# The fourth token sum split by quarters, and the down weights loaded through ScalarE's queue

## The reference, cut to what matters

```python
def conv_ffn(h, w_in, conv_w, conv_b, w_out):
    u = h @ w_in                       # 1024 x 1024 times 1024 x 5632, the up-projection
    u = causal depthwise convolution of width 3 over the tokens (u, conv_w) + conv_b
    gate, val = jnp.split(u, 2, axis=-1)
    return (jax.nn.gelu(gate, approximate=True) * val) @ w_out   # 2816 wide, the down-projection
x = x + rmsnorm(conv_ffn(rmsnorm(x, g[2]), ...), g[3])
```

## Time and profile before

| | |
|---|---|
| median of three runs | 2400.64 us (2400.22 to 2401.5) |
| profiled execution, span from first to last instruction | 2401.0 us |
| TensorE busy | 2298.9 us, 96% |
| VectorE busy | 1747.0 us, 73% |
| ScalarE busy | 1194.4 us, 50% |
| POOL busy | 835.0 us, 35% |
| mean granted TensorE clock | 0.979 |
| up-projection with the fourth sum, layer 0 / layer 1 | around 822 / 1811 us |
| start of the down-projection, layer 0 / layer 1 | around 1190 / 2180 us |

### The profile page before, as it was taken

How to read it: one execution, slowest core, us unless ns; L and a number is a source line. 1 busy time by engine, 2 the same in 40 slices (tenths; PEclk the granted TensorE clock), 3 DMA queues, 4 the chain that set the end, 5 groups by cost and what they waited for, 6 DMA issues and landing times. The chain is left out here.

```text
span 2401.0 us, 31689 instructions
## 1 busy us (share of the span) xinstructions
PE 2298.9 (96%) x11379; PEld 1925.4 (80%) x11379; DVE 1747.0 (73%) x2659; ACT 1194.4 (50%) x1967; POOL 835.0 (35%) x605
## 2 busy tenths in 40 slices
PE   6899979989999999999999989999999999999998
PEld 5678768889888788888878867788887888887886
DVE  5576677865554788888899854555568888888986
ACT  5457777666543444344444643355533434434454
POOL 2112103301010678877500001132147787880000
PEclk9999989999999999999999999989999999999999
DMA  5111100000152122222473531041222222228435
GB/s 149 36 27 49 31 18 27 28 1 1 38 174 80 59 82 79 88 79 79 145 259 119 171 131 40 16 111 47 71 79 79 79 83 93 79 75 279 160 118 185
DMA packets 189062, 212.84 MB, mean 89 GB/s; under 512 B 14788, under 2 KB 135972, under 8 KB 188908
## 3 DMA queue, kind: packets, MB, share of 16 engines
q1 hardware_dynamic: 184156, 193.51, 25.5%
q10 hardware_dynamic: 4752, 17.30, 1.8%
HBM read 170.83 MB, written 39.94 MB: 88 GB/s over the span
## 5 line engine op out<-in xcount | busy, mean ns | idle before, releaser
L126 PE MATMUL trunk_ps<-l_bhi,l_ahi 128*128 128x512 f32 x528 | 206.6, 391 | 5.7 <-DVE l_blo L2799 5.5
L126 PE MATMUL trunk_ps<-l_bhi,l_alo 128*128 128x512 f32 x528 | 205.6, 389 | 0.0
L126 PE MATMUL trunk_ps<-l_blo,l_ahi 128*128 128x512 f32 x528 | 205.5, 389 | 0.0
L126 PE MATMUL trunk_ps<-l_t_lo,l_s_hi 128*128 128x512 f32 x456 | 177.4, 389 | 0.0
L126 PE MATMUL trunk_ps<-l_t_hi,l_s_hi 128*128 128x512 f32 x456 | 177.4, 389 | 0.0
L126 PE MATMUL trunk_ps<-l_t_hi,l_s_lo 128*128 128x512 f32 x456 | 177.4, 389 | 0.0
L2427 POOL TENSOR_TENSOR l_s_lo<-l_raw,l_s_hi 128x512 fp32r<-128x512 f32 x90 | 160.4, 1791 | 43.0 <-ACT l_s_hi L2333 43.0
L2209 ACT ACTIVATE l_ahi<-l_a 128x512 fp32r<-128x512 f32 x132 | 83.0, 629 | 135.9 <-PE trunk_ps L126 131.0
L2427 POOL TENSOR_TENSOR l_s_lo<-l_w_sum,l_s_hi 128x512 fp32r<-128x512 f32 x76 | 120.0, 1581 | 48.1 <-ACT l_s_hi L2333 48.1
L209 POOL TENSOR_TENSOR wring_w_lo<-wring_raw,wring_w_hi 128x1024 fp32r<-128x1024 f32 x22 | 52.6, 2394 | 228.0 <-ACT wring_w_hi L205 228.0
L126 PEld LDWEIGHTS trunk_ps<-l_bhi,l_ahi 128*128 128x128 f32 x528 | 99.1, 188 | 30.9 <-DVE l_alo L2796 6.1
(11 more groups left out here) (476 smaller groups left out, 6766.1 us busy)
## 6 DMA issues: line engine op xcount, KB each, us to landing
l_draw<-in_ffn_w_out SPq DMA_DIRECT2D x154, 256.0 KB, 2.8
l_raw<-in_ffn_w_in SPq DMA_DIRECT2D x48, 512.0 KB, 4.7
gated_dram<-l_gate_out SPq DMA_DIRECT2D x44, 512.0 KB, 2.6
l_a<-gated_dram SPq DMA_DIRECT2D x88, 256.0 KB, 4.1
wring_raw<-in_even_w_in SPq DMA_DIRECT2D x20, 512.0 KB, 3.9
l_raw_g<-in_ffn_w_in SPq DMA_DIRECT2D x20, 512.0 KB, 3.8
l_raw_v<-in_ffn_w_in SPq DMA_DIRECT2D x20, 512.0 KB, 4.9
l_wt<-in_ffn_w_out SPq DMA_DIRECT2D x22, 256.0 KB, 5.8
```

What stands on the lines that cost most here:

```text
L126: mm = pe.matmul(o, w, m, start=a, stop=z, skip_group_check=onto)
```

## The change

Three edits, all in `trunk_stage`, which runs once per layer.

1. The fourth token sum's high part is made by ScalarE in four copies of 128x512. On ScalarE, the copies `hi(4)` and `hi(5)` go ahead of the gate tap of pair 2; after them come a wait for all six up tiles, the four quarter copies and `hi(6)`; the gate tap, GELU and value tap of pair 2 follow.
2. VectorE makes the low part in four subtractions, `fourth_lo(k)`: two ahead of the gate taps of pair 2, two between its gate and its value taps. Product A22 of round 0 waits for the fourth of them.
3. The 11 slices of `wt` are loaded by ScalarE's DMA queue, two after each of `step_hi(5)` to `step_hi(9)` and the last after `step_hi(10)`, where SyncE issued one after each row from 7 to 17.

```diff
@@ sync
-                    if 7 <= q < 7 + DT:
-                        load_wt(q - 7)
@@ scalar
+                def load_wt(j):
+                    if j == 0:
+                        sc.wait_ge(product_done, NP - 2)
+                    if j >= 4:
+                        sc.wait_ge(wt_in[j % 4], 16 * (j // 4))
+                    sc.dma_start(wt[:, j, :], wo[(DT + j) * P:(DT + j + 1) * P, H[1]]).then_inc(wt_in[j % 4], 16)
@@
                 tap_last("v", 1)
-                hi(1)
-                hi(2)
-                hi(3)
+                for m in range(1, 6):
+                    hi(m)
+                sc.wait_ge(tile_done, NT_UP)
+                for k in range(QUARTER):
+                    sc.wait_ge(t_sum, 4 * (k + 1))
+                    sc.activation(t_hi[4][:, k, :], t4_sum[:, k, :], ACT.Copy).then_inc(t4_hi_done, 1)
+                hi(6)
                 tap_last("g", 2)
-                hi(4)
                 gelu(2)
-                hi(5)
                 tap_last("v", 2)
-                hi(6)
-                sc.wait_ge(x_sum, 4 * QUARTER)
-                sc.wait_ge(t_sum, 4 * QUARTER)
-                sc.activation(t_hi[4], t4_sum[:], ACT.Copy).then_inc(t4_hi_done, 1)
@@
                 for q in range(5, steps_of(P2)):
                     step_hi(q)
+                    for j in range(2 * (q - 5), min(DT, 2 * (q - 4))):
+                        load_wt(j)
@@ tensor, product(m)
                     if r == 0 and q == A22:
-                        pe.wait_ge(t4_lo_done, 1)
+                        pe.wait_ge(t4_lo_done, QUARTER)
@@ vector
+                def fourth_lo(k):
+                    dve.wait_ge(t4_hi_done, k + 1)
+                    dve.tensor_tensor(t_lo[4][:, k, :], t4_sum[:, k, :], t_hi[4][:, k, :].bitcast(F32), ALU.subtract).then_inc(t4_lo_done, 1)
@@
                 gate(1)
+                fourth_lo(0)
+                fourth_lo(1)
                 taps("g", 2)
+                fourth_lo(2)
+                fourth_lo(3)
                 taps("v", 2)
                 gate(2)
-                dve.wait_ge(t4_hi_done, 1)
-                dve.tensor_tensor(t_lo[4], t4_sum[:], t_hi[4].bitcast(F32), ALU.subtract).then_inc(t4_lo_done, 1)
-                dve.wait_ge(t4_lo_done, 1)
+                dve.wait_ge(t4_lo_done, QUARTER)
                 weight_sums(1)
```

More of the change, by code:

```diff
@@ L2064, in load_row @@
                     sp.dma_start(raw_ring[q % NR][:], wo[r * P:(r + 1) * P, c]).then_inc(row_in[q % NR], 16)
[L2066 to L2071, removed]
                 def load_quarter(i):
```

## The result

| | before | after |
|---|---|---|
| median of four runs each, taken together | 2401.07 us (2400.22 to 2402.6) | 2413.26 us (2409.66 to 2413.37) |
| profiled execution, span | 2401.0 us | 2411.3 us |
| mean granted TensorE clock | 0.979 | 0.980 |

The changed kernel is slower: ratio 1.0041, 95% interval 1.0028 to 1.0054, about 10 us. The two traced executions differ by 10.3 us and the medians by 12.2: in all other runs the time stands 1.7 to 2.1 us above the span, so the traced execution of before, at about 2402.9, was slower than the four listed, and its span of 2401.0 isn't the 0.4 us above the median that the prediction took it for. The forecast had 2406.1 and a range that ended at 2409.5; it had the direction and missed the size.

A forecast was written before the change was run, and what follows sets the result against it. TensorE, busy 96% of the span, was taken as the bound, so only its standstills count. The terms 0.9 + 2.9 + 1.7 = +5.5 us on the median 2400.64 gave 2406.1 us, range 2396.5 to 2409.5.

The forecast's parts named there:

- The stall moves from A22 to A12, because hi(5) waits for POOL: Up-projection, round 0: 3.55 and 3.95 us lost at A12 where 3.12 and 3.51 were lost at A22.
- the step that I bounded: POOL's low part of A12, layer 0: 1.29 us alone, 2.16 beside a gate multiplication, taken as 1.8.
- The quarter subtractions and A22 cost nothing: Up-projection, round 0: quarter subtractions fit into VectorE's hole and between taps; A22 no longer waits, with 0.7 us to spare.
- The low clock of the up-projection is kept: Half clock after the stall, moved by two products and otherwise kept; if it stayed away, 1.7 us a layer are won.
- Weight sums of round 1 ... no wait, or a few tenths: VectorE's sums begin at about 842.5 instead of 841.4; round 1's second product waits not at all or a few tenths.
- part 1's +0.4 a layer: Up-projection: the loss at A12 exceeds the former loss at A22 by 0.4 us in each layer.
- Row 11 is late by two more weights, 1.44 us a layer: Down-projection: six weights instead of four share the DMA engines ahead of row 11, +1.44 us a layer, TensorE likewise.
- rows earlier: Down-projection rival: row 11, issued sooner, lands sooner, 4.1 us in favour; 2397.4 with the up-projection's +0.9; chance 0.20.
- The low clock after step 10: Down-projection: layer 0's stall of 4.2 us brings a low clock, +1.7 us; layer 1's 3.1, on the edge, left out.
- everything late: Rival: weights 8 and 9 also delay, low clocks in both layers, +10, 2410.6; chance within the forecast and late variants' 0.50.
- 2.8 us on weights 8 and 9: Down-projection: these two weights may also delay row 11, up to 1.4 us more; 2.8 in the rival everything late.

The follow-up runs named there:

- Experiment 2: The run of e3: kernel before with the fourth sum by quarters, but hi(5) behind pair 2's GELU; down weights as before. Ratio 0.9998 to the kernel before.
- experiments 3 and 4: e8, which is e3 with ScalarE's hi(5), hi(6) and VectorE's weight sums moved ahead: 0.9957; e11, the changed kernel with VectorE's move alone: 1.0045.
- e2: Kernel before with only the down weights moved to ScalarE's queue, the fourth sum split whole as before: ratio 1.0033, 7.9 us slower.
- e11: Changed kernel with VectorE's weight sums of round 1 moved ahead of pair 2's value taps and gate multiplication: ratio 1.0045 to the kernel before.
- Experiments 5 and 6: e6 and e7 move 32 of 512 columns in each down-weight load (2402.48 and 2398.09 us); e4 changes the order of weights on ScalarE's queue (0.9984).
- the down part alone: The run e2: kernel before with only the down weights moved to ScalarE's queue: ratio 1.0033, 7.9 us slower.
- Experiment 7: The run of e10: changed kernel with 12 useless matmuls ahead of the last three of step 9 in each layer. Ratio 1.0024 to the kernel before.
- e10: Changed kernel with 12 more matmuls, into banks overwritten later, ahead of the last three of step 9: ratio 1.0024 to the kernel before.
- e4: As e2, but weight slices 0 to 3 go out after step 5 and the others one a step from step 11: ratio 0.9984 to the kernel before.
- e6: As e2, but each down-weight load moves 32 of its 512 columns, leaving out part of the work: 2402.48 us in one run.
- e7: Kernel before, down weights on SyncE's queue, with each of their loads moving 32 of 512 columns, leaving out part of the work: 2398.09 us in one run.
- e1: Kernel before with only the fourth sum by quarters and its edits on ScalarE, VectorE and TensorE; down weights on SyncE's queue: ratio 1.0012, 2.9 us slower.
- e3: Kernel before with the fourth sum by quarters, hi(5) behind pair 2's GELU and hi(6) behind its value tap; down weights as before: ratio 0.9998.
- e8: As e3, with hi(5), hi(6) ahead of pair 2's GELU and round 1's weight sums ahead of its value taps: ratio 0.9957 to the kernel before.

## Why the prediction was right in most of its mechanisms and wrong in its size

By parts, the forecast had +0.9 for the first and +4.6 (2.9 and 1.7 of clock) for the second; alone they measured 2.9 and 7.9.

- **The stall moves from A22 to A12, because hi(5) waits for POOL.** Right. Forecast 3.55 and 3.95 us lost at A12; the starts give 838.91 - 824.23 - 10.88 = 3.80 in layer 0 and 1831.29 - 1816.22 - 10.88 = 4.19 in layer 1. The 0.25 missing came from the step that I bounded: I put POOL's slowing into the low part of A12 (1.8), which took 1.29; it fell on the sum S4, 2.08 instead of 1.29, beside the gate multiplication, itself 2.14 instead of 1.23. The Trainium skill, page "GPSIMD Engine Reference", section "Specifications", says that POOL shares its SBUF interfaces with VectorE and contends with VectorE instructions that have two SBUF inputs. The trace agrees in that 2.08 and 2.14 overlap; but the low part of A12 ran beside the same gate multiplication and kept its 1.29, so the slowing can't be told from the overlap alone.
- **The quarter subtractions and A22 cost nothing.** Right: no wait is left at A22.
- **The low clock of the up-projection is kept.** Too low: in layer 0 it lasted 6.8 us instead of 3.4. This is most of TensorE's 1.64 us there, of which the longer stall is 0.68.
- **"Weight sums of round 1 ... no wait, or a few tenths".** TensorE's first waits were judged rightly, but the wrong consumer was asked. The consumer that counts is the store of the last gated tile, 360 us later. It is set by the later one of two: the elementwise loop, which began 1.26 us later in layer 0, and TensorE, 1.64 us later with 0.85 us of slack, 0.8 us net. The measured 1.02 lies between; in layer 1 the loop began 1.27 us later and the store came 1.33 later. Experiment 2 shows the loop's limit on its own, experiments 3 and 4 TensorE's. The prediction has no such term: I carried part 1's +0.4 a layer into the sum as if TensorE's delay passed through; 0.8 became 2.35.
- **Row 11 is late by two more weights, 1.44 us a layer.** Right: 1.53 and 1.98, with some luck in how near. The same placing gave 0.47 and 1.39 in e2 and 0.80 and 1.90 in e11; the six have a mean of 1.35. Experiments 5 and 6 show that it is the bytes ahead of it. The second queue's weights do take turns with the row: in the kernel after slice 8 is issued 2.6 and 2.0 us behind row 11 and lands with it, 17.83 and 17.14 us after the store against the row's 17.72 and 17.46. The Trainium skill, page "DMA: Bandwidth & Descriptors", section "Issuing engines are not separate DMA queues", says that DMAs started by several engines run on the same 16 DMA engines and save only issue time. The trace agrees: in the 11 us from 5.45 us behind the store on, the DMA share is 1.00 with 350 GB/s after, with both queues loading, against 1.03 and 364 before. The rival "rows earlier" failed twice. It had row 11 issued 2.4 us sooner; in layer 0 it was issued 9.40 us after the store instead of 8.36. The ring of four didn't hold it: row 7's low part was made at 1211.27, 2.8 us ahead of the issue at 1214.07. It stood in SyncE's queue behind two quarters, issued from 1213.22 on, and the first of them waits for the quarter four before it, which landed at 1213.16. So taking the weights out of the queue left another landing in front of the row. In layer 1 it did go out sooner, 8.45 instead of 9.33, and was used 9.10 us behind its issue instead of 6.24. An earlier issue bought nothing there.
- **The low clock after step 10, "taken once".** This is the step of the prediction that failed most. It took +1.7 in layer 0 and left layer 1 out as on the edge, at a wait of 3.1 us. Measured: 2.66 + 1.55 = 4.2 us, in both layers and over 6.8 us in layer 0. Layer 1's wait was 3.92 and not 3.1: to before's 1.66 come 1.98 by row 11 and 1.33 by the store, less 1.05 by which TensorE itself came later. The sum had 1.44 for row 11 and asked neither when the store nor when TensorE comes. That layer 1 was no edge case doesn't hang on the store: the down part alone waited 3.81 us there with the store on time. Experiment 7 takes this term away and gets 4.1 us back by the ratio (2.8 by the traces).

The rival "everything late" (2410.6) had low clocks in both layers and a total of +10, which is the total measured, but for another reason in part: it put 2.8 us on weights 8 and 9, where row 11 was only 0.1 and 0.5 later than the 1.44, and on the store no more than the 0.4 a layer.

What stays open: why the low stretch lasts 6.8 us once and 3.4 another time, and how much of 10 us against 5.5 in the runs is owed to that. It differs behind nearly the same wait (at A12 of layer 1, 3.4 us in the kernel after and 6.8 in e10 and e11, behind 4.04, 4.08 and 4.07), so single traces can't price it.

## What to carry to other kernels

Ask of a removed stall who is next in time, and not only on the same engine: here the elementwise loop ran beside TensorE at nearly the same period, and a gain of 3.7 us for TensorE alone was worth nothing until that loop also began earlier. Where a later wait ends one chain (a store and the loads behind it) and is reached by another (TensorE), price both ends of it in one sum, and add the clock: here every wait over 3 us at A12 and at step 10 brought the low one. A second DMA queue gave here another order of the bytes and no more bandwidth: send what can go into the empty time before the gate (here the store), and nothing between it and the row that is waited for.

## What the runs showed of the hardware that I had not expected

- The same wait doesn't always bring the same clock. At A22 of layer 1 a wait of 3.35 us was followed by a low stretch before, and so in e4 and e6 (3.36 and 3.35); the same instruction was followed by none in e7 (3.37) and in e2:

```profile
1830.01 0.47 PE L126 MATMUL trunk_ps<-odd_act_hi,l_s_hi 128*128 128x512 f32 x1 [3.35 <-DVE odd_act_lo L2913]
```

```profile
1829.50:1834.00 4.50, 3.99 (x18) 3.33 (x19) 2.05 (x4) 1.46 (x3) 2.54 (x2) 1.00 0.22 90
```

- In these traces a wait of 2.05 us at step 10 was followed by a low stretch in two kernels (e1 in layer 0, e3 in layer 1), one of 2.10 (e1 in layer 1), one of 2.54 (e8) and one of 2.84 by none. Of those at A12 and step 10 above 3 us all 15 were, and none of the waits at step 10 up to 1.7 us.
- A low stretch behind these waits lasted 3.4 us or twice that. The six of 6.8 us behind A12 (in e1, e10, e11 and the kernel after) and the two behind step 10 (the kernel after, e2) followed waits of 3.2 to 4.1 us, but a ninth, behind A22 in e6, followed one of 2.96. Step 10 in layer 0 of the kernel after takes 5.3 us in it instead of 2.8.
- 12 matmuls without use, in a wait that is there anyway, were cheaper than the low clock behind it (experiment 7).
